# Output projection of a hybrid decoder layer: two blocks by two in seven half-size products

## What is computed

```python
h = _rmsnorm(x, norm_g[l])
proj = jnp.einsum('bsd,de->bse', h, w_in[l])
xa, ga, q, ckv, gb, qi, ki, wi = jnp.split(proj, IN_SPLITS, axis=-1)
ya = _rglru_branch(xa, ...) * jax.nn.silu(ga)      # conv, two gates, linear recurrence
yb = _dsa_branch(q, ckv, qi, ki, wi, ...) * jax.nn.silu(gb)   # top-256 attention, 8 heads
y = jnp.concatenate([ya, yb], axis=-1)             # 1024 x 2048
x = x + jnp.einsum('bse,ed->bsd', y, w_out[l])     # w_out is 2048 x 2048
return _rmsnorm(x, final_norm_g)
```

## Time and profile before

| | |
|---|---|
| median of 3 runs | 1501.9 us (1501.67 to 1502.22) |
| the profiled execution, its own time | 1500.5 us |
| its span | 1498.6 us |
| mean granted TensorE clock | 0.999 |
| PE busy | 1478.4 us, 99% |
| DVE busy | 874.1 us, 58% |
| POOL busy | 648.1 us, 43% |
| ACT busy | 618.3 us, 41% |

### The profile page before, as it was taken

How to read it: one execution, slowest core, us unless ns; L and a number is a source line. 1 busy time by engine, 2 the same in 40 slices (tenths; PEclk the granted TensorE clock), 3 DMA queues, 4 the chain that set the end, 5 groups by cost and what they waited for, 6 DMA issues and landing times.

```text
span 1498.6 us, 20944 instructions
## 1 busy us (share of the span) xinstructions
PE 1478.4 (99%) x7512; PEld 1314.1 (88%) x7512; DVE 874.1 (58%) x1516; ACT 618.3 (41%) x833; POOL 648.1 (43%) x461
## 2 busy tenths in 40 slices
PE   8999999999999999999999999999999999999997
PEld 7889999988888888888888888888888888888886
DVE  6478666587777897778666544587777000050003
ACT  7345555444345445332211111265655233333540
POOL 4355545445655555654444444200002444454650
PEclk9999999999999999999999999999999999999999
DMA  8222111022221222325423222344334633346422
GB/s 282 83 54 80 43 49 42 22 64 88 77 72 61 67 73 87 99 86 180 168 91 97 92 91 84 121 156 156 124 106 162 239 102 108 99 164 258 141 84 112
DMA packets 142528, 163.54 MB, mean 109 GB/s; under 512 B 9494, under 2 KB 106888, under 8 KB 140424
## 3 DMA queue, kind: packets, MB, share of 16 engines
q1 hardware_dynamic: 140936, 158.59, 32.6%
q0 software_dynamic: 1536, 4.20, 0.9%
HBM read 126.58 MB, written 36.18 MB: 109 GB/s over the span
## 4 chain that ended last, share of the span: by engine, by line
PE 81%; issue 8%; POOL 5%; DVE 4%; ACT 1%; DMA 0%; POOLq 0%; DVEq 0%; SPq 0%; ACTq 0%
PE ps L1243 18%; PE ps L1244 18%; PE ps L1245 18%; POOL wo_lo L869 5%; PE ps L1482 4%; PE ps L1496 3%; PE ps L1498 3%; PE ps L1497 3%; PE ps L1363 2%; PE ps L1365 2%; PE ps L1463 2%; PE ps L1587 1%; PE ps L1585 1%; PE ps L1586 1%; PE ps L1255 1%
## 5 line engine op out<-in xcount | busy, mean ns | idle before, releaser
L1243 PE MATMUL ps<-hT_hi,w_lo 128*128 128x512 f32 (+1 forms) x1344 | 496.4, 369 | 0.0
L1244 PE MATMUL ps<-hT_lo,w_hi 128*128 128x512 f32 (+1 forms) x1344 | 495.8, 369 | 0.0
L1245 PE MATMUL ps<-hT_hi,w_hi 128*128 128x512 f32 (+1 forms) x1344 | 495.8, 369 | 0.0
L841 POOL TENSOR_TENSOR w_lo<-w_raw,w_hi 128x512 fp32r<-128x512 f32 x168 | 235.7, 1403 | 429.7 <-ACT w_hi L933 429.7
L1243 PEld LDWEIGHTS ps<-hT_hi,w_lo 128*128 128x128 f32 x1344 | 254.1, 189 | 29.9
L1244 PEld LDWEIGHTS ps<-hT_lo,w_hi 128*128 128x128 f32 x1344 | 254.1, 189 | 29.6
L1245 PEld LDWEIGHTS ps<-hT_hi,w_hi 128*128 128x128 f32 x1344 | 254.0, 189 | 29.2
L933 ACT ACTIVATE w_hi<-w_raw 128x512 fp32r<-128x512 f32 x168 | 105.6, 629 | 405.2 <-PE ps L1245 251.1
L839 POOL TENSOR_TENSOR w_raw<-w_raw,g_col 128x512 f32<-128x512 f32 x168 | 210.5, 1253 | 36.1 <-DMA w_raw<-in_w_in 36.1
L1966 DVE TENSOR_TENSOR res<-ps,res 128x512 f32<-128x512 f32 x32 | 21.8, 690 | 274.0 <-PE ps L1498 226.6
L869 POOL TENSOR_TENSOR wo_lo<-wo_raw,wo_hi 128x1024 fp32r<-128x1024 f32 x48 | 118.1, 2461 | 137.4 <-ACT wo_hi L1133 137.4
(11 more groups left out here) (216 smaller groups left out, 1908.3 us busy)
## 6 DMA issues: line engine op xcount, KB each, us to landing
w_raw<-in_w_in SPq DMA_DIRECT2D x168, 256.0 KB, 2.8
wo_raw<-in_w_out SPq DMA_DIRECT2D x64, 512.0 KB, 3.7
xin<-in_x SPq DMA_DIRECT2D x8, 1024.0 KB, 7.2
res<-in_x SPq DMA_DIRECT2D x8, 1024.0 KB, 11.4
out<-res SPq DMA_DIRECT2D x16, 512.0 KB, 3.9
...
```

The source lines that it names most:

```text
L841: nc.gpsimd.tensor_tensor(w_lo[:, j, :, :], part, w_hi[:, j, :, :].bitcast(F32), ALU.subtract).then_inc(w_lo_s, 1)
L1243: nc.tensor.matmul(o, wlo, hi, start=(kt == 0), stop=False)
L1244: nc.tensor.matmul(o, whi, lo, start=False, stop=False)
L1245: return nc.tensor.matmul(o, whi, hi, start=False, stop=(kt == KT - 1))
```

## The change

w_out is cut into 2 x 2 blocks (features by columns, 1024 x 1024 each), and y into 2 x 2 quarters (tokens by features). The result's quarters come from seven products of such blocks in place of eight, in the form with few additions: product 1 is a11 b11, 2 is a12 b21, and products 4, 6, 7, 5, 3 have a sum or difference as one or both factors. Each product is two chunks of 512 columns (CHUNKS = 14), each over eight feature blocks: 14 x 8 x 4 x 3 = 1344 matmuls, where there were 8 x 16 x 4 x 3 = 1536. A piece of weights is now one feature block, 128x512, and wo_hi and wo_lo have three buffers each.

- *Differences of weights* (`differences`, on POOL): from b11, b12, b21, b22 four differences are made in place in four tiles tw of 128x512. One such unit (four loads, four subtractions, four stores to t_dram) is done for each of 8 feature blocks and 2 column halves: 16 units. They stand in the recurrent stage, one in each tile from turn 1 on, and two in the first pair of attention tiles: POOL makes them between the pieces 1 and 2 of a tile, SP loads and stores them between weight loads. tw lies in the memory of wuk, so the load of wuk moves behind the last store.
- *Sums of activations* (`made`, `made_low` on DVE, `high_s` on ACT): in the output stage a quarter of hT that is no longer needed is replaced by a sum or difference of quarters: DVE joins high and low of both (two additions), combines them, ACT rounds the result, DVE subtracts for low. 4 x 8 of these.
- *Sums of products*: DVE adds each finished bank to one or two of twelve result tiles (rt, ra: 128x1024), among which x is loaded. The upper left quarter is stored to c11_dram and loaded back near the end, for want of room; the pieces of the last chunk are mixed into those of the two before it.
- *The end*: the lower tokens are normalised while chunk 13 runs, now by eight steps of 1024 columns and one root for four row blocks; the upper tokens after it.

The diff, cut to its core:

```diff
-OCH = D // OC
-OPK = 2
-OP = KT // OPK
-HALF_T = 4
-CHUNKS = 2 * OCH
-EARLY = [(0, 0), (0, 1)]
+KH = KT // 2
+NQ = 4
+NHALF = D // 2
+PRODUCTS = [1, 4, 2, 6, 7, 5, 3]
+PLACE = {1: (0, 0), 4: (KH, NT), 2: (KH, 0), 6: (KH, NT), 7: (0, NT), 5: (0, 0), 3: (KH, 0)}
+CHUNKS = 2 * len(PRODUCTS)
+LASTC = CHUNKS - 1
+ORDER = [(c, m) for c in range(CHUNKS - 3) for m in range(KH)]
+for c in (CHUNKS - 3, CHUNKS - 2):
+    for m in range(0, KH, 2):
+        ORDER += [(c, m), (c, m + 1), (LASTC, (c - CHUNKS + 3) * NQ + m // 2)]
+RANK = {cm: r for r, cm in enumerate(ORDER)}
+EARLY = [(m, q) for m in range(2) for q in range(2)]
...
+            def t_load(m, p):
+                for n, (k0, e0) in enumerate(((0, 0), (0, NHALF), (KH, 0), (KH, NHALF))):
+                    sp.dma_start(tw[n][:, :], w_k[ds(m + k0, 1), :, e0 + p * OC:e0 + (p + 1) * OC].rearrange(
+                        "o p e -> (o p) e")).then_inc(t_in, 16)
+
+            def t_store(m, p):
+                sp.wait_ge(t_sub, m * 8 + 4 * p + 4)
+                for n, i in enumerate((0, 3, 1, 2)):
+                    sp.dma_start(t_d[n, p, ds(m, 1)].rearrange("o p e -> (o p) e"), tw[i][:, :]).then_inc(t_st, 16)
+
+            def lru_pair(g, first=False):
+                weights(T_LRU + 2 * g, COL_XA + g * P, js=range(3))
+                if not first:
+                    t_store(g - 2, 1)
+                weights(T_LRU + 2 * g, COL_XA + g * P, js=[3])
+                if not first:
+                    sp.wait_ge(t_st, g * 128 - 128)
+                t_load(g - 1, 0)
+                weights(T_LRU + 1 + 2 * g, COL_GA + g * P, js=range(3))
+                t_store(g - 1, 0)
+                weights(T_LRU + 1 + 2 * g, COL_GA + g * P, js=[3])
+                sp.wait_ge(t_st, g * 128 - 64)
+                t_load(g - 1, 1)
                 gate_loads(g)
                 y_stores(g - 1)
+
...
-            att_loads(0)
+            weights(T_ATT, COL_Q, js=range(3))
+            t_store(G - 2, 1)
+            weights(T_ATT, COL_Q, js=[3])
+            sp.wait_ge(t_st, 128 * (G - 1))
+            t_load(G - 1, 0)
+            weights(T_ATT + 1, COL_GB, js=range(3))
+            t_store(G - 1, 0)
+            weights(T_ATT + 1, COL_GB, js=[3])
+            sp.wait_ge(t_st, 128 * (G - 1) + 64)
+            t_load(G - 1, 1)
+            y_stores(G - 1)
+            weights(T_ATT + 2, COL_Q + P, js=range(3))
+            t_store(G - 1, 1)
+            weights(T_ATT + 2, COL_Q + P, js=[3])
+            sp.wait_ge(t_st, 128 * G)
             sp.dma_start(wuk[:, :, :], a["w_uk"][0].rearrange("h d c -> d h c")).then_inc(wuk_in, 16)
...
+            def differences(u):
+
+                b11, b12, b21, b22 = (b[:, :] for b in tw)
+                pool.wait_ge(t_in, u * 64 + 64)
+                nc.gpsimd.tensor_tensor(b11, b12, b11, ALU.subtract).then_inc(t_sub, 1)
+                pool.wait_ge(t_sub, u * 4 + 1)
+                nc.gpsimd.tensor_tensor(b12, b22, b12, ALU.subtract).then_inc(t_sub, 1)
+                pool.wait_ge(t_sub, u * 4 + 2)
+                nc.gpsimd.tensor_tensor(b22, b22, b11, ALU.subtract).then_inc(t_sub, 1)
+                pool.wait_ge(t_sub, u * 4 + 3)
+                nc.gpsimd.tensor_tensor(b21, b22, b21, ALU.subtract).then_inc(t_sub, 1)
+
+            def low(t, unit=None):
                 for j in range(PIECES):
+                    if j == 2 and unit is not None:
+                        differences(unit)
...
-                low(g * 2 + T_LRU)
-                low(g * 2 + (T_LRU + 1))
+                low(g * 2 + T_LRU, g * 2 - 2)
+                low(g * 2 + (T_LRU + 1), g * 2 - 1)
                 low_y(g - 1)
-            low(T_ATT)
-            low(T_ATT + 1)
+            low(T_ATT, 2 * G - 2)
+            low(T_ATT + 1, 2 * G - 1)
...
+            def high_s(i, m):
+
+                n = i * KH + m
+                places, free = ((a21, 0), (a22, 3 + 4 * KH), (a11, 3 + 2 * KH), (a12, 3 + 6 * KH))[i]
+                act.wait_ge(s_made, n + 1)
+                if free:
+                    act.wait_ge(wo_used, free)
+                nc.scalar.activation(places[m][0], g0[:, (n % 2) * NT:(n % 2 + 1) * NT], ACT.Copy).then_inc(s_hi, 1)
+
+            S_AFTER = {-1: (0, 0), 0: (0, 4), 3: (1, 0), 4: (1, 4), 5: (2, 0), 6: (2, 4), 8: (3, 0), 9: (3, 4)}
+            for c, m in ORDER[2:]:
+                out_high(c, m)
+                if c == LASTC:
+                    continue
+                if m >= 5 and c - 1 in S_AFTER:
+                    i, m0 = S_AFTER[c - 1]
+                    high_s(i, m0 + m - 5)
...
+            def out_rows(c, m, q):
+                s0, t0 = PLACE[PRODUCTS[c // 2]]
+                tok = slice(t0 + q * P, t0 + (q + 1) * P)
+                o = banks(c % 2, q)
+                whi, wlo = (woven_out(w) for w in wo_cut(c, m))
+                nc.tensor.matmul(o, hT_lo[:, s0 + m, tok], whi, start=(m == 0), stop=False)
+                nc.tensor.matmul(o, hT_hi[:, s0 + m, tok], wlo, start=False, stop=False)
+                return nc.tensor.matmul(o, hT_hi[:, s0 + m, tok], whi, start=False, stop=(m == KH - 1))
...
+            def made(i, m):
+
+                n = i * KH + m
+                (xh, xl), (yh, yl), op = ((a11[m], a21[m], ALU.subtract), (a22[m], a21[m], ALU.subtract),
+                                          (a22[m], a11[m], ALU.add), (a12[m], a22[m], ALU.subtract))[i]
+                ta, tb_ = g0[:, (n % 2) * NT:(n % 2 + 1) * NT], g1[:, (n % 2) * NT:(n % 2 + 1) * NT]
+                if n > 1:
+                    dve.wait_ge(s_lo, n - 1)
+                step.did(tt(ta, xh.bitcast(F32), xl.bitcast(F32), ALU.add))
+                chain(tt(tb_, yh.bitcast(F32), yl.bitcast(F32), ALU.add))
+                tt(ta, ta, tb_, op).then_inc(s_made, 1)
+
+            def made_low(i, m):
+
+                n = i * KH + m
+                hi, lo = (a21, a22, a11, a12)[i][m]
+                dve.wait_ge(s_hi, n + 1)
+                tt(lo, g0[:, (n % 2) * NT:(n % 2 + 1) * NT], hi.bitcast(F32), ALU.subtract).then_inc(s_lo, 1)
+
+            def four_made(i, m0):
+                made(i, m0)
+                for m in range(m0, m0 + 4):
+                    if m + 1 < m0 + 4:
+                        made(i, m + 1)
+                    made_low(i, m)
...
+            inverse_root(NQ, NQ, 1)
             dve.wait_ge(gf_in, 32)
-            for half in range(2):
-                dve.wait_ge(res_in, 64 * (half + 1))
-                with dve.Fori(0, OCH // 2 - 1) as i:
-                    for u in range(2):
-                        add_residual(i * 2 + (OCH * half + u), i * 2 + u, u)
-                add_residual(OCH * half + OCH - 2, OCH - 2, 0)
-                add_residual(OCH * half + OCH - 1, OCH - 1, 1, half)
+            for q in range(NQ):
+                for r, g in ((r_two, g0), (r_one, g1)):
+                    scaled(r[q][:, :], r[q][:, :], NQ + q, g[:, :])
+            add_chunk(12)
+            dve.wait_ge(c11_in, 16 * NQ)
+            for q in range(NQ):
+                add_products(LASTC, q)
+                dve.wait_ge(o_sq, 1 + 7 * NQ + q + 1)
+                inverse_root(q, 1, 2 + q)
+                dve.wait_ge(out_21, 16 * NQ)
+                scaled(r_two[q][:, :].rearrange("p (k e) -> p k e", k=2), c11_back[q], q,
+                       g0[:, :].rearrange("p (k e) -> p k e", k=2))
+                scaled(r_u[q][:, :], r_u[q][:, :], q, g1[:, :])
```

More of the change, by code:

```diff
@@ L298, in layer @@
         pu = ExitStack()
+        tw = [alloc(pu)(f"tw{i}", [P, OC]) for i in range(4)]
+        pu.close()
+        pu = ExitStack()
         wuk = alloc(pu)("wuk", [P, NH, C])
@@ L511, in layer @@
         f_out = sem("f_out")
-        out_st = [sem(f"out_st{q}") for q in range(HALF_T)]
+        out_21 = sem("out_21")
+        out_st = sem("out_st")
         act_step = sem("act_step")
@@ new lines, in _ @@
+            sp.wait_ge(x12_used, 4)
+            for part, half in ((g0, left), (g1, right)):
+                sp.dma_start(part[:, :], a["final_norm_g"][half].rearrange("(o d) -> o d", o=1).broadcast_to(
+                    [P, NHALF])).then_inc(gf_in, 16)
+            for q in range(NQ):
+                sp.wait_ge(f_out, 2 * q + 1)
+                sp.dma_start(out[0, rows(NQ + q), left], r_two[q][:, :]).then_inc(out_21, 16)
+                sp.wait_ge(f_out, 2 * q + 2)
+                sp.dma_start(out[0, rows(NQ + q), right], r_one[q][:, :]).then_inc(out_st, 16)
@@ L797, in _ @@
+            for q in range(NQ):
+                sp.wait_ge(f_out, 2 * NQ + 2 * q + 1)
+                sp.dma_start(out[0, rows(q), left], r_two[q][:, :]).then_inc(out_st, 16)
+                sp.wait_ge(f_out, 2 * NQ + 2 * q + 2)
+                sp.dma_start(out[0, rows(q), right], r_u[q][:, :]).then_inc(out_st, 16)
+            sp.wait_ge(out_21, 16 * NQ)
+            sp.wait_ge(out_st, 16 * 3 * NQ)
         @block.gpsimd
@@ L1222, in _ @@
+            root_mean(NQ, NQ, 1)
+            for q in range(NQ):
+                square_rows(12, q)
```

(30 more changed lines are left out.)

429 lines of the change are left out of this document (227 added, 202 removed).

## The result

The changed kernel takes **1578.9 us** (median of 4 runs, 1578.5 to 1579.2) against 1501.8 before (1501.7 to 1502.2): ratio 1.051, interval 1.049 to 1.053. The forecast was 1541, range 1510 to 1566: the direction and the place were right, but the loss was 77 us and not 39, twice the size, and the time lies outside the range.

A forecast was written before the change was run, and what follows sets the result against it. A ring of ACT, POOL and SP (43.6 us) was taken to run beside PE's 44.0 us turn. Profiled 1500.5 - 41.4 (output matmuls) + 1.0 (tail) + 79.3 (71.7 subtractions, 7.6 wuk) = 1539.4, 1541 against the median; range 1510 to 1566.

The forecast's parts named there:

- The ring beside PE: Recurrent stage: a chain of ACT, POOL and SP beside PE needs 43.6 of a turn's 44.0 us.
- Turns 54 to 55 us apart: Recurrent stage, sign named for the profile after: ACT's sigmoid table loads 54 to 55 us apart, not 44.
- The wait for data in the xa tile: Recurrent stage, xa tile: POOL's subtractions wait 0.8 us for their loaded data, bounds 0 and 3.
- The subtractions: Recurrent stage: four POOL subtractions of 1.28 us per unit; net +4.9 us in the ga tile, +6.2 in the xa tile.
- The contention rule: Recurrent stage: POOL and DVE clash when DVE has two SBUF inputs, so only the ga unit can be slowed.
- wuk: End of the recurrent stage: wuk's load, moved behind the last stores, makes PE wait +7.6 us before the transposes.
- the lower clock: Recurrent stage: PE's idle stretches of about 4 us may lower its clock; nothing added, PE having 10 us a turn spare.
- The output stage: Output stage: 192 fewer matmuls at 0.2158 us, -41.4 us, all on the path.
- the cover: Output stage: three buffers leave two pieces, 5.2 us, for a hand-over of 2.3; stalls taken as 0.
- The tail: After the last matmul: DVE is free later but wins back 0.5 us a row, 2.5 - 1.5 = +1.0 us.
- That the subtractions are hidden: Rival, recurrent stage: POOL's idle time absorbs the subtractions and the time falls to 1461 us; chance 0.07.
- The stall of the output stage: Rival, output stage: ACT waits for DVE's sums, 5 us in each of eight chunks, +40, 1581 us; chance 0.07.

The follow-up runs named there:

- experiment 2: Changed kernel with tw loaded once and the subtractions kept in place, no later loads or stores for them, output stage reading w_out: 1547.6 us, one run.
- Experiment 3: Changed kernel with the units' loads, stores and waits kept but no subtractions made: 1496.5 us, one run.
- experiment 4: Changed kernel with SP's two y stores moved behind the four weight loads of the next xa tile: 1527.4 us, one run.
- experiment 5: Kernel before the change with only SP's y stores moved behind the weight loads of the next xa tile: 1500.4 us, one run.
- experiment 8: Changed kernel, y stores behind weight loads, second unit's subtractions on the fourth ga and first three xa pieces, last unit's loads early: 1476.6 us, ratio 0.984.
- Experiment 1: Changed kernel without difference units in the recurrent stage, wuk loaded at its old place, all pieces read from w_out: 1468.4 us, ratio 0.978.
- experiment 7: Changed kernel, y stores behind weight loads, subtractions placed in POOL's waits for ACT, three tail scaling steps moved into DVE's waits: 1474.0 us, ratio 0.981.
- experiment 9: As experiment 8, with three of DVE's eight scaling steps of the lower tokens moved into its waits in the last chunk: 1472.3 us, ratio 0.981.
- experiment 10: As experiment 9, with each difference stored once made and the second unit's subtractions ending one piece earlier, on the second xa piece: 1465.1 us, ratio 0.975.
- experiment 11: As experiment 1, with three of DVE's eight scaling steps of the lower tokens moved into its waits in the last chunk: 1466.1 us, ratio 0.977.

## Why the prediction was right or wrong

**The ring beside PE: right.** It was read from the earlier trace rows, and experiments 2 to 5 each changed one of its members. *Turns 54 to 55 us apart* was the sign named; the table loads are 58.3 apart, and ACT no longer waits for PE at any of them.

**The wait for data in the xa tile: the term that failed.** It was put at 0.8 us (its own times, 451.0 - 450.45, give 0.55) with bounds of 0 and 3, and is 4.05. The landing times were taken from w_raw's 2.8, but four stores or loads of the same size in a row are there 3.9 us after the last store's issue and 4.2 after the last load's, one after the other, since a load waits for the stores: 2.5 us. SP's issues up to the last store took 4.0 us and those of the loads 1.9, where 3.3 and 1.6 were counted: 1.0 us more. Experiment 3, with the transfers and no subtraction, shows the wait alone to cost 4.1 us a turn. The bound of 3 had no row behind it; the nearest rows on both sides, 2.8 and wuk's 5.5, taken for both landings, would have given some 0.6 and 6.0.

**The subtractions: right in size.** 1.28 us each (taken from w_lo) and 0.08 between; the first one in the ga tile took 2.26 beside DVE's product, so that unit costs 6.3 us and not 5.9. The turn's sum, 43.6 + 6.2 + 4.9 = 54.7, lacks 3.2 of waiting and 0.4 here, and with them is 58.3. PE ended the last tile 98.9 us late, apart from the 1.3 at the start, and not 71.7: 27.2 us more, which is seven to eight turns of 3.6. The lower bound has a slip: subtractions of 1.04 us and no wait are 4.4 + 4.4 - 1.0 - 0.4 = 7.4 us a turn, not 7.0, so it should have stood some 3 us higher.

**The contention rule** stood behind a row, and the runs bear it out both ways. POOL's subtractions and w_lo are slow beside DVE's products and not beside its top-8 rounds; in experiment 8 it was DVE's product that was slowed (2.32 us for 1.22). The Trainium skill, GPSIMD Engine Reference, section 1 (Specifications), says that the two share their SBUF interfaces, with contention when a DVE instruction has two SBUF inputs or runs in a 2-port mode; these numbers agree with the first condition. The prediction left the second out (the output stage, below, has a case that may be of that kind).

**wuk: right, and one thing missed.** PE waited 8.5 us (7.6 forecast). Its transposes behind that wait took 3.68 us and not the 1.91 of the earlier trace rows, close to twice, as the lower of the clock's two levels, 1.2 GHz, would have it, and the granted clock of the 50 us from there was 0.96: the lower clock was priced at nothing because PE had time to spare in the turns, but at their end it had none.

**The output stage: a little short.** The price of the matmuls was right, but PE's way from the transposes to the last matmul shrank by 34.8 us and not 41.4. Of the 6.6, 1.8 are the slow transposes, and some 0.5 the first matmuls behind them. PE waited 3.7 us in the last four chunks for wo_lo, where the cover was taken as enough; before, it waited 1.0. PE's waits from 1500 us on, a window there, and ACT's timeline in it:

```profile
PE ps L1602 <- POOL wo_lo L976: 3.7, 4, 1.5
...
1512.00:1522.00 10.00, 9.00 (x43) 1.00 1.00 360
...
1522.76 0.90 ACT L1236 ACTIVATE hT_hi<-wo_raw 128x512 fp32r<-128x512 f32 x1 [6.00 <-DMA wo_raw<-in_w_out]
```

(The window has only PE, the granted clock, the DMA engines' share and GB/s.) It was not POOL or ACT that were late but the weights: two loads of x, the four of the spilled quarter (issued from 1511.83) and two more of x stand on SP among the pieces there, each of 512 KB, and from 1512 to 1522 us the DMA engines were busy all the time. The 10 us of sums cost nothing.

Another 1.0 us was lost just ahead of the output stage. POOL makes the first wo_lo there. A piece is now half as large, and POOL begins 0.7 us earlier in the attention's last steps, at the same moment as a scaling by DVE that PE waits for. The changed kernel, and below it the same scaling before:

```profile
1255.82 1.30 POOL L976 TENSOR_TENSOR wo_lo<-wo_raw,wo_hi 128x512 fp32r<-128x512 f32 x1 [5.61 <-ACT wo_hi L1236]
1255.86 1.61 DVE L1976 TENSOR_SCALAR prob_sb<-prob_sb,sums 128x640 f32<-128x640 f32 x1
1257.52 0.77 PE L1573 MATMUL ps<-ident,prob_sb 128*128 128x128 f32 x5 [0.98 <-DVE prob_sb L1976]
```

```profile
1145.03 0.55 DVE L1875 TENSOR_SCALAR prob_sb<-prob_sb,sums 128x640 f32<-128x640 f32 x1
```

Experiment 1 has the same 1.61 us and the same wait of 0.98. That POOL is what slowed it is read from the times; no run moved the one and kept the other. What is left of the 6.6, under 1 us, was not traced.

**The tail: right in kind, short in size.** +1.0 was forecast and +4.2 came. The eight steps were to begin 5 us ahead of chunk 12's end (1543.8 here); they began at 1542.30, behind ACT's squares and root and the load of final_norm_g. DVE's timeline:

```profile
1542.30 1.28 DVE L2123 SCALAR_TENSOR_TENSOR ra<-ra,fstat,rt 128x1024 f32<-128x1024 f32 x1 [1.00 <-DMA rt<-in_final_norm_g]
...
1568.90 0.68 DVE L2110 TENSOR_TENSOR rt<-ps,rt 128x512 f32<-128x512 f32 x1
```

The last addition starts 4.6 us after the last matmul (1564.27). Three of the steps moved into DVE's waits bring the way from the end of that matmul to the end of the span down to between 8.3 and 8.6 us (experiments 7, 9, 10 and 11), where it is 12.0 in the changed kernel and 7.9 in the one before.

**The rivals.** That the subtractions are hidden would have been 1461; hidden they are only in other places (experiment 10, 1465.1), not in these. The stall of the output stage, 1581 us, came near the measured time by another way: experiment 1 has no such stall of 40 us, only the few us above. The upper end of the range, 1566, allowed 3 us more a turn for slower subtractions *or* late data; the two came to 3.6, and the tail, the clock and the output stage, each taken near nothing, added another 10. The late data by themselves would have put the time near the upper end of the range; it took these smaller terms as well to leave it.
